# The first projection stage in three token pieces, with two operand buffers and squares summed on GpSimd

## The reference

```python
xn = rms_norm(h, norm_g)
z = xn @ w_in                      # 2048 x 11392
zs = z[..., :D_SHIFT]              # 25 tiles of 128 columns
zs_mix = zs + (zs_prev - zs) * shift_mu
...
ya = (y * jax.nn.silu(g_r)) @ w_proj_a
...
yb = (u * s * jax.nn.silu(g_g)) @ w_proj_b
m = jax.nn.sigmoid(gate_a) * ya + jax.nn.sigmoid(gate_b) * yb
return h + m @ w_out, new_shift, S, vn
```

## Time and profile before

| | us |
|---|---|
| median of three runs | 3621.11 |
| the profiled execution | 3622.61 |
| its span | 3620.9 |
| PE busy over the span | 3439.6 (95%) |
| DVE, ACT, POOL busy | 1756.8, 1152.7, 883.1 |
| `phase_front`, from the start to the first transfer of `phase_mix` | 0 to 843.5 |

### The profile page before, as it was taken

The page is one execution under the profiler, slowest core; times in us unless marked ns, Lnnn a source line. Parts: engine busy times, 40 slices in busy tenths (PEclk is TensorE's granted clock), DMA queues, the critical chain, the costliest instruction groups (busy, mean ns, idle before and its releaser), DMA issues. The chain is left out here.

```text
span 3620.9 us, 60687 instructions
## 1 busy us (share of the span) xinstructions
PE 3439.6 (95%) x25742; PEld 3329.3 (92%) x25742; DVE 1756.8 (49%) x2100; ACT 1152.7 (32%) x1325; POOL 883.1 (24%) x1494
## 2 busy tenths in 40 slices
PE   8999999996999999899999899999786799999998
PEld 7999999996999999899999899999774799999997
DVE  6333233223555555555555655555236455554653
ACT  2000000002444444544444444443224333433432
POOL 0000000001444444344434344444014003103112
PEclk9999999998999999999999999999798899999999
DMA  4111111114545545554545454554344555555564
GB/s 165 72 70 60 68 72 72 61 50 157 156 137 147 148 136 156 143 144 140 147 138 149 145 151 138 148 147 140 99 134 159 187 175 171 179 194 177 184 209 137
DMA packets 338449, 494.35 MB, mean 137 GB/s; under 512 B 219762, under 2 KB 282754, under 8 KB 306308
## 3 DMA queue, kind: packets, MB, share of 16 engines
q1 hardware_dynamic: 325364, 460.64, 41.1%
q10 hardware_dynamic: 12240, 28.77, 2.1%
q0 software_dynamic: 576, 1.08, 0.1%
HBM read 412.49 MB, written 77.90 MB: 135 GB/s over the span
## 5 line engine op out<-in xcount | busy, mean ns | idle before, releaser
L511 PE MATMUL st_acc<-st_xh,st_wh 128*128 128x364 f32 (+1 forms) x2688 | 914.9, 340 | 36.8 <-DVE st_wl L471 27.5
L511 PE MATMUL st_acc<-st_xh,st_wl 128*128 128x364 f32 (+1 forms) x2688 | 888.9, 331 | 0.0
L511 PE MATMUL st_acc<-st_xl,st_wh 128*128 128x364 f32 (+1 forms) x2688 | 887.8, 330 | 0.0
L511 PEld LDWEIGHTS st_acc<-st_xh,st_wh 128*128 128x128 f32 x2688 | 511.8, 190 | 46.5 <-issue 22.7
L471 DVE TENSOR_TENSOR st_wl<-st_raw,st_wh 128x2048 fp32r<-128x2048 f32 x168 | 395.8, 2356 | 259.9 <-ACT st_wh L441 259.8
L511 PEld LDWEIGHTS st_acc<-st_xh,st_wl 128*128 128x128 f32 x2688 | 511.1, 190 | 2.0
L511 PEld LDWEIGHTS st_acc<-st_xl,st_wh 128*128 128x128 f32 x2688 | 510.5, 190 | 0.0
L441 ACT ACTIVATE st_wh<-st_raw 128x2048 fp32r<-128x2048 f32 x168 | 321.5, 1914 | 420.4 <-PE st_acc L511 418.0
L175 PE MATMUL fr_acc<-fr_xh,fr_wh 128*128 128x364 f32 x1584 | 355.1, 332 | 1.5 <-issue 1.5
L175 PE MATMUL fr_acc<-fr_xl,fr_wh 128*128 128x364 f32 x1584 | 349.4, 329 | 0.0
L175 PE MATMUL fr_acc<-fr_xh,fr_wl 128*128 128x364 f32 x1584 | 349.1, 328 | 0.0
(11 more groups left out here) (213 smaller groups left out, 5212.2 us busy)
## 6 DMA issues: line engine op xcount, KB each, us to landing
st_raw<-in_w_in SPq DMA_DIRECT2D x168, 1024.0 KB, 5.3
tl_raw<-in_w_proj SPq DMA_DIRECT2D x48, 1024.0 KB, 5.1
tl_raw<-in_w_out SPq DMA_DIRECT2D x48, 1024.0 KB, 4.9
fr_raw<-in_w_in SPq DMA_DIRECT2D x33, 1024.0 KB, 4.8
z<-st_stage SPq DMA_DIRECT2D x168, 182.0 KB, 5.5
z<-fr_stage ACTq DMA_DIRECT2D x33, 548.0 KB, 2.7
tl_gate<-z SPq DMA_DIRECT2D x64, 192.0 KB, 2.5
zrk<-z SPq DMA_DIRECT2D x68, 128.0 KB, 5.6
```

Source lines behind the costliest of these rows:

```text
L511: mm = pe.matmul(self.acc[s][:, w], wt[s][:, k * P:(k + 1) * P], x[:, k, w], start=(k == 0 and wt is self.wh and x is self.xh), stop=(k == ...
```

## The change

`phase_front` is written anew. The tokens are taken in three pieces of 364, 364 and 360, and for each piece all 33 tiles are computed, so there are 99 units of 48 matmuls, and each weight tile is loaded and split three times. A unit has one PSUM bank; there are two accumulators. `xh` and `xl` exist twice, for the piece in use and the next. The blocks of `x` of the next piece are loaded and split during every second unit (tiles 0, 2, ... 30). The high parts of weights and of `x` are made on ACT (`high`, `x_high`), the low parts on DVE (`low`, `x_low`). The squares are taken on ACT, summed on POOL, and one matmul per piece gives the mean. There are three stage buffers. The stores to `z` (182 KB, without the first four columns) are issued on SP's queue, between the loads of weights. The last column of a piece is kept in `edge` for the next one. `rstd` is stored at the end. Later phases are not changed.

```diff
--- before.py
+++ after.py
-        xh = sc.sb("fr_xh", [P, KT, TP], F32R)
-        xl = sc.sb("fr_xl", [P, KT, TP], F32R)
-        gm = Gemm(nc, sc, "fr", wt, KT, xh, xl, (0, 0))
...
+        W, R, PIECES = 364, 4, ((0, 364), (364, 364), (728, 360))
+        NP, NU = len(PIECES), len(PIECES) * NFRONT
+        two = lambda name, shape, dt=F32: [sb(f"fr_{name}{s}", shape, dt) for s in range(2)]
+        xh, xl = two("xh", [P, KT, W], F32R), two("xl", [P, KT, W], F32R)
+        raw, wh, wl = two("raw", [P, KT * P]), two("wh", [P, KT * P], F32R), two("wl", [P, KT * P], F32R)
...
+        stage = [sb(f"fr_stage{n}", [P, ZO + W]) for n in range(3)]
+        aux, ssq, rstd = sb("fr_aux", [P, W]), sb("fr_ssq", [P, W]), sb("fr_rstd", [P, TP])
...
+        acc = [sc.ps(f"fr_acc{s}", [P, 512]) for s in range(2)]
+        ms = sc.ps("fr_ms", [P, 512])
...
+        next_x = lambda u: (piece(u) + 1, tile(u) // 2) if piece(u) + 1 < NP and tile(u) % 2 == 0 and tile(u) < 2 * KT else None
...
+                def load_w(u):
+                    after(sp, lo_ready, u - 1)
+                    sp.dma_start(raw[u % 2][:, :], wt[tile(u)]).then_inc(w_loaded[u % 2], 16)
+
+                def load_x(q, k):
+                    n = q * KT + k
+                    after(sp, x_ready, n - R + 1)
+                    after(sp, sq_ready, n - R + 1)
+                    sp.dma_start(ring[n % R][:, wd(q)], xT[k, :, span(q)]).then_inc(x_loaded[n % R], 16)
...
+                for k in range(1, KT):
+                    load_x(0, k)
+                    if k == 3:
+                        load_w(1)
...
+                for u in range(NU):
+                    if u + 2 < NU:
+                        load_w(u + 2)
+                    if next_x(u):
+                        load_x(*next_x(u))
+                    sp.wait_ge(out_ready, u + 1)
+                    sp.dma_start(z[tile(u), :, span(piece(u), ZO)], zs(u)).then_inc(stored[u % 3], 16)
+                sp.dma_start(rstd_dram, rstd[:, :]).then_inc(extra_stored, 16)
...
+                for q in range(NP):
+                    for k in range(KT):
+                        n = q * KT + k
+                        pool.wait_ge(sq_ready, n + 1)
+                        if k == 0:
+                            after(pool, ms_done, q)
+                            pool.tensor_copy(ssq[:, wd(q)], sq[n % 2][:, wd(q)]).then_inc(ssq_ready, 1)
+                        else:
+                            pool.wait_ge(ssq_ready, n)
+                            pool.tensor_tensor(ssq[:, wd(q)], ssq[:, wd(q)], sq[n % 2][:, wd(q)], ADD).then_inc(ssq_ready, 1)
...
+                def high(u):
+                    act.wait_ge(w_loaded[u % 2], 16 * (u // 2 + 1))
+                    after(act, group_done, u - 1)
+                    nc.scalar.activation(wh[u % 2][:, :], raw[u % 2][:, :], ACT.Copy).then_inc(hi_ready, 1)
+
+                def x_high(q, k):
+                    n = q * KT + k
+                    act.wait_ge(x_loaded[n % R], 16 * (n // R + 1))
+                    after(act, group_done, (q - 1) * NFRONT)
+                    nc.scalar.activation(xh[q % 2][:, k, wd(q)], ring[n % R][:, wd(q)], ACT.Copy,
+                                         scale=g_sb[:, k:k + 1]).then_inc(xh_ready, 1)
+                    after(act, ssq_ready, n - 1)
+                    nc.scalar.activation(sq[n % 2][:, wd(q)], ring[n % R][:, wd(q)], ACT.Square).then_inc(sq_ready, 1)
+
+                def root(q):
+                    act.wait_ge(ms_done, q + 1)
+                    nc.scalar.activation(rstd[:, span(q)], ms[:, wd(q)], ACT.Sqrt, bias=eps[:, 0:1]).then_inc(rt_ready, 1)
...
+                act.wait_ge(const_ready, 4)
+                act.wait_ge(g_loaded, 16)
+                for k in range(KT):
+                    x_high(0, k)
+                    if k == 0:
+                        high(0)
+                root(0)
+                high(1)
+                for u in range(NU):
+                    if u + 2 < NU:
+                        high(u + 2)
+                    if next_x(u):
+                        x_high(*next_x(u))
+                    if tile(u) == NFRONT - 1 and piece(u) + 1 < NP:
+                        root(piece(u) + 1)
+                    if tile(u) >= N_SHIFT:
+                        act.wait_ge(evacuated, u + 1)
+                        after(act, out_ready, u)
+                        nc.scalar.activation(aux[:, wd(piece(u))], zs(u), ACT.Sigmoid).then_inc(sig_ready, 1)
...
+                def x_low(q, k):
+                    n = q * KT + k
+                    dve.wait_ge(xh_ready, n + 1)
+                    dve.scalar_tensor_tensor(xl[q % 2][:, k, wd(q)], ring[n % R][:, wd(q)], g_sb[:, k:k + 1],
+                                             xh[q % 2][:, k, wd(q)].bitcast(F32), MUL, SUB).then_inc(x_ready, 1)
...
+                def evacuate(u):
+                    q, g = piece(u), tile(u)
+                    dve.wait_ge(group_done, u + 1)
+                    dve.wait_ge(rstd_ready, q + 1)
+                    after(dve, stored[u % 3], 16 * (u // 3))
+                    dve.tensor_tensor(zs(u), acc[u % 2][:, wd(q)], rstd[:, span(q)], MUL).then_inc(evacuated, 1)
+                    if g >= N_SHIFT:
+                        return
+                    n = shifted(u)
+                    dve.tensor_copy(stage[u % 3][:, ZO - 1:ZO], edge[:, g:g + 1]).then_inc(first_ready, 1)
...
+                for u in range(NU):
+                    if u and tile(u) == 0:
+                        reciprocal(piece(u))
+                    evacuate(u)
+                    if u + 2 < NU:
+                        low(u + 2)
+                    if next_x(u):
+                        x_low(*next_x(u))
+                    if tile(u) >= N_SHIFT:
+                        dve.wait_ge(sig_ready, gates(u) + 1)
+                        dve.tensor_tensor(zs(u), zs(u), aux[:, wd(piece(u))], MUL).then_inc(out_ready, 1)
...
+                for u in range(NU):
+                    q, s = piece(u), u % 2
+                    pe.wait_ge(lo_ready, u + 1)
+                    after(pe, evacuated, u - 1)
+                    for k in range(KT):
+                        if tile(u) == 0:
+                            pe.wait_ge(x_ready, q * KT + k + 1)
+                        for w, x in ((wh, xh), (wl, xh), (wh, xl)):
+                            mm = pe.matmul(acc[s][:, wd(q)], w[s][:, k * P:(k + 1) * P], x[q % 2][:, k, wd(q)],
+                                           start=(k == 0 and w is wh and x is xh), stop=(k == KT - 1 and x is xl))
+                    mm.then_inc(group_done, 1)
+                    if u == 0:
+                        mean_square(0)
+                    if tile(u) == NFRONT - 1 and q + 1 < NP:
+                        mean_square(q + 1)
...
```

More of the change, by code:

```diff
@@ new lines, in phase_front @@
+        diff_ready, fixed_ready, sh_ready = sem("fr_diff_ready"), sem("fr_fixed_ready"), sem("fr_sh_ready")
+        sig_ready, out_ready, extra_stored = sem("fr_sig_ready"), sem("fr_out_ready"), sem("fr_extra_stored")
+        piece, tile = lambda u: u // NFRONT, lambda u: u % NFRONT
+        wd = lambda q: slice(0, PIECES[q][1])
+        span = lambda q, at=0: slice(at + PIECES[q][0], at + PIECES[q][0] + PIECES[q][1])
+        zs = lambda u: stage[u % 3][:, ZO:ZO + PIECES[piece(u)][1]]
+        shifted = lambda u: piece(u) * N_SHIFT + min(tile(u), N_SHIFT)
@@ L223, in phase_front @@
+        gates = lambda u: piece(u) * (NFRONT - N_SHIFT) + max(tile(u) - N_SHIFT, 0)
+        AT = PROMPT - PIECES[-1][0]
+        last_col = slice(ZO + AT - 1, ZO + AT + SAMPLE, STEPS)
+        first_of_seq = lambda at: slice(at + AT, at + AT + SAMPLE, STEPS)
+        next_x = lambda u: (piece(u) + 1, tile(u) // 2) if piece(u) + 1 < NP and tile(u) % 2 == 0 and tile(u) < 2 * KT else None
         with nc.Block() as block:
@@ L243, in _ @@
                 sp.wait_ge(extra_stored, 32)
+                for n in range(3):
+                    sp.wait_ge(stored[n], 16 * ((NU + 2 - n) // 3))
             @block.gpsimd
@@ L317, in _ @@
             @block.tensor
             def _(pe):
-                pe.wait_ge(const_ready, 1)
-                def sum_squares(n):
-                    pe.wait_ge(sq_ready, n + 1)
-                    for c in range(3):
-                        mm = pe.matmul(gm.acc[1][:, c, 0:NCH], ones[:, :], sqb[n % 2][:, c * NCH:(c + 1) * NCH],
-                                       start=(n == 0), stop=(n == KT - 1))
-                    mm.then_inc(sq_summed, 1)
-                gm.products(pe, 0, 0, sum_squares)
@@ L330, in _, with mean_square @@
-                pe.wait_ge(rt_ready, 1)
-                for g in range(1, NFRONT):
-                    gm.products(pe, g // 2, g % 2)
+                def mean_square(q):
+                    pe.wait_ge(ssq_ready, (q + 1) * KT)
+                    after(pe, rt_ready, q)
+                    pe.matmul(ms[:, wd(q)], ones[:, :], ssq[:, wd(q)], start=True, stop=True).then_inc(ms_done, 1)
```

(8 more changed lines are left out.)

130 lines of the change are left out of this document (41 added, 89 removed).

## The result

The kernel after takes 3672.59 us, the median of four runs (3671.69 to 3676.18); the kernel before takes 3621.14 beside it. The ratio is 1.0142, with a 95% interval of 1.013 to 1.0153: 51.4 us slower. The profiled execution has a span of 3670.9 us, 50.0 more than before. The forecast was 3654 (3636 to 3680).

What follows compares the result with a forecast made beforehand. PE's matmuls bound the first stage. From the profiled 3622.6 us, -16.0 (start and matmuls) + 49.7 (waits for weights) - 1.0 (end) = +32.7 gave 3655.3, with the median 1.5 lower: 3654 us, range 3636 to 3680.

Steps and rivals of the forecast that it cites:

- Start: First stage, before unit 1: 16 blocks of `x`, then mean square, root and split; unit 1 starts near 40.0 us.
- the block of `x`: x phase: `x_low` on DVE 0.62 plus POOL's sum 0.86, with hand-overs 1.5 us for each further block.
- Mutual exclusion of POOL and DVE: x phase and even units: POOL's sum and DVE's work exclude each other; without it the forecast is some 11 us lower.
- Pace: PE's matmuls in the 98 units after unit 0: 166.0 ns each, 7.97 and 7.89 us per unit.
- Ring: Gate tiles: landing, splits, product, store, next load take 10.35 or 11.8 us against PE's 7.97; 49.7 us lost.
- the landing: Load of 1 MB of weights, issue to arrival: taken as 5.1 us; loss 43.4 with 4.8, 61 with 5.6.
- Rival (c): Loads slow down as the stage's traffic rises to about 160 GB/s: landing 5.6 to 6.0, 3665 to 3674 us; 15%.
- Rival (b): PE falls to half clock in the gaps and stays there: 80 us more, 3734 us; chance 4%.
- the window row: Profile before, cited against half clock in gaps of this size: PE busy 8.59 of 10 us kept clock 1.00.
- End: From the stage's last result to the next phase: 6.7 us against 7.66 before, a gain of 1 us.
- Later phases: Phases after the first stage: untouched by the change, so no difference in time.
- the clock falls in the stage: Sign in the first stage's PE clock that, if seen, would make the prediction wrong; no size given.

Runs made afterwards that it cites:

- sums_on_dve: Kernel after with gate tiles' sigmoid and product ahead of the next unit's split, and the squares summed on DVE instead of POOL; 3603.9 us, 0.9955 to the kernel before.
- load_ahead: Kernel after with each load of weights issued one turn of SP's list earlier; 3607.7 us, 0.9962 to the kernel before.
- after_again: The kernel after, unchanged, measured a second time; 3668.3 us, 1.013 to the kernel before.

## Why the prediction was right

The direction, the place and the mechanism were right, and the time lay in the range. By spans, step by step (predicted +32.7, measured +50.0):

- **Start.** Unit 1 starts at 35.77, not at 40.0 (the terms given for it add up to 39.4). The mis-sized term is the block of `x`: 1.22 us, not 1.5. The 0.86 of the earlier trace rows in it is a sum of 320 columns (the one at 3603.1, with DVE idle), and none of 364 columns stands alone in a trace; in sums_on_dve `x_low` takes 0.59. Of a pair of at least 0.86 and 0.59 only 1.22 is seen, so the two overlap for 0.2 us or more. Half clock in unit 1 gave 1.7 back. Unit 1 is taken up at 45.72, where 40.0 + 8.24 follows from the prediction (7.97, and 0.27 to the take-up, as at tile 1 before: 24.26 against 23.99): -2.5.
- **Mutual exclusion of POOL and DVE.** Held in kind: 1.22 us per block against 0.97 with both on DVE, 0.7 us for each sum in the ring, and an `x_low` of 1.31 behind POOL's 2.19. The Trainium skill has the rule under "SBUF — State Buffer", section "SBUF: two separate sides"; the trace agrees that they take turns, while a lock over each whole instruction would give 1.45 or more, which no block shows.
- **Pace.** 8.00 and 7.91 us per unit, taken as 7.97 and 7.89: +2.5.
- **Ring.** 61.5 instead of 49.7: 24.0, 25.1 and 12.4 at the piece ends instead of 20.4, 20.5 and 8.8. The mis-sized term is the landing: 5.6 us from issue to the next high part (mean of 21, 5.1 to 6.3), not 5.1. By the prediction's own 2.1 us per 0.1 that is +10.3. The engines' part of the ring was shorter than predicted (5.08 and 6.31 us, not 5.25 and 6.7), which takes about 4 back, and the half clock of the last late units adds 5.5. Together 61.5, so the prediction's "61 with 5.6" came true because the last two nearly cancel. Rival (c) had the landing, but for a reason that did not hold: the prediction laid 0.3 us on the store ahead of the load, and load_ahead shows 0.5 with less traffic.
- **Half clock.** Rival (b) said that with half clock in a unit's first few us only "nothing is lost". That statement failed. In the middle of the ring it holds, since the ring runs past PE. But the last late unit of each piece has nothing late behind it: against 8.31 and 8.22 us at full clock (after_again) they took 9.84, 10.63 and 9.75, so about 1.5, 2.4 and 1.5 us stay. They are 5.5 of the 61.5, and only 1.5 of the 57.3 in after_again. The Trainium skill, "TensorE: Matmul & The Clock Gate", section "HAM oscillation", warns of it for a PE that waits for transfers; against the window row on which it was set aside, these traces agree with it, in the clocks 0.91 to 0.94 of the piece ends.
- **End.** 6.9 us instead of 6.7, against 7.66 before.
- **Later phases.** +5.2, predicted 0. Over the 13 profiles of this study they scatter from 2774.6 to 2782.6 with the same code, so this is put down to no step of the change.

The sum: -2.5 + 2.5 + 11.8 + 0.2 + 5.2 = +17.2, the difference between 32.7 and 50.0 to 0.1. The median is 18.6 us above the forecast: it was not below the profiled execution this time, as the prediction took from before. That start and pace cancel is luck, and so is the close fit of the ring's sum.

What the profile was to show is there: gaps only at tiles 29 to 32 and 0 to 2, put down to the low part (0.6 to 4.7 us, and none at tile 30 of the first piece, where half clock fills it); the high part waiting for the load; sums well over 0.86 us. One sign named as fatal came up, "the clock falls in the stage": it does, for some 15% of the piece ends' time (a granted clock of 0.91 to 0.94 is half clock for 12 to 18%), and the mechanism stood all the same. As a test it was drawn too wide.
